# Reweaving the first mixer of a two-block fp32 network on one Trainium2 core

## The reference

```
mod = silu(c) @ w_ada + b_ada              # 6 vectors of 1024: shift1 scale1 gate1 shift2 scale2 gate2
h   = rms_norm(x, norm1_w) * (1 + scale1) + shift1
p   = h @ w_in
qkv = silu(causal_depthwise_conv(p[q, k, v columns], 4 taps))     # 4 heads of 128 each
g, beta = from two small groups of columns of p
o   = gated_delta_rule_chunked(l2_normalize(q), l2_normalize(k), v, g, beta)   # 8 chunks of 64 tokens
y_gdn = rms_norm(o, gdn_norm_w) * silu(z)                          # the output gate, 4 heads
y_sc  = sc_b * causal_depthwise_conv(sc_c * sc_h, 3 taps)          # short convolution half
x   = x + gate1 * (concatenate([y_gdn, y_sc]) @ w_out)
x   = x + gate2 * swiglu(rms_norm(x, norm2_w) * (1 + scale2) + shift2)
```

## Time and profile before

| | us |
|---|---|
| median of 3 runs | 2214.73 |
| the profiled execution, its own time | 2213.37 |
| its span, first to last instruction | 2212.1 |
| PE busy in the span | 2030.4 |
| DVE, ACT, POOL busy | 815.9, 694.8, 764.5 |
| mean granted clock of TensorE | 0.950 |

### The profile page before, as it was taken

How to read it: one execution, slowest core, us unless ns; L and a number is a source line. 1 busy time by engine, 2 the same in 40 slices (tenths; PEclk the granted TensorE clock), 3 DMA queues, 4 the chain that set the end, 5 groups by cost and what they waited for, 6 DMA issues and landing times. The chain is left out here.

```text
span 2212.1 us, 32165 instructions
## 1 busy us (share of the span) xinstructions
PE 2030.4 (92%) x13960; PEld 1697.1 (77%) x13960; DVE 815.9 (37%) x1075; ACT 694.8 (31%) x1048; POOL 764.5 (35%) x444
## 2 busy tenths in 40 slices
PE   3878999699999999999999888889999799999997
PEld 2656777578888889999999888776666577888885
DVE  5767362421111112443310266644444334444201
ACT  2342111343222233222222323344454324222222
POOL 2322120144444465344445432311111144444453
PEclk9988998799999999999999999889998999999999
DMA  7322221423333323323223422100000132333231
GB/s 266 133 96 77 77 77 39 135 76 103 92 93 92 97 86 96 96 89 93 84 90 93 130 67 72 39 6 2 1 2 2 64 118 86 96 95 95 88 95 64
DMA packets 55627, 182.76 MB, mean 83 GB/s; under 512 B 7456, under 2 KB 7712, under 8 KB 55360
## 3 DMA queue, kind: packets, MB, share of 16 engines
q1 hardware_dynamic: 55488, 180.72, 25.5%
HBM read 175.45 MB, written 5.24 MB: 82 GB/s over the span
## 5 line engine op out<-in xcount | busy, mean ns | idle before, releaser
L2076 POOL TENSOR_TENSOR WL<-RAWS,WH 128x1024 fp32r<-128x1024 f32 (+2 forms) x275 | 650.0, 2365 | 1032.2 <-ACT WH L1609 1032.2
L480 PE MATMUL PS<-HH,WH 128*128 128x264 f32 (+2 forms) x2184 | 681.8, 354 | 37.3 <-DVE HL L1028 7.5
L480 PE MATMUL PS<-HL,WH 128*128 128x264 f32 (+2 forms) x2184 | 661.4, 345 | 0.0
L480 PE MATMUL PS<-HH,WL 128*128 128x264 f32 (+2 forms) x2184 | 659.0, 344 | 0.0
L480 PEld LDWEIGHTS PS<-HH,WH 128*128 128x128 f32 (+1 forms) x2184 | 383.4, 193 | 106.6 <-issue 37.6
L1609 ACT ACTIVATE WH<-RAWS 128x1024 fp32r<-128x1024 f32 (+2 forms) x275 | 283.7, 1033 | 444.7 <-PE PS L480 429.4
L480 PEld LDWEIGHTS PS<-HH,WL 128*128 128x128 f32 (+1 forms) x2184 | 383.5, 193 | 49.2 <-issue 0.4
L480 PEld LDWEIGHTS PS<-HL,WH 128*128 128x128 f32 (+1 forms) x2184 | 383.8, 193 | 48.5 <-issue 3.4
L480 PE MATMUL PS<-IHf,WH 128*128 128x512 f32 (+1 forms) x704 | 209.4, 338 | 0.0
L480 PE MATMUL PS<-IHf,WL 128*128 128x512 f32 (+1 forms) x704 | 209.3, 338 | 0.0
L480 PE MATMUL PS<-ILf,WH 128*128 128x512 f32 (+1 forms) x704 | 209.2, 338 | 0.0
(11 more groups left out here) (499 smaller groups left out, 1981.1 us busy)
## 6 DMA issues: line engine op xcount, KB each, us to landing
RAWS<-w_w_in SPq DMA_DIRECT2D x52, 512.0 KB, 4.4
RAWS<-w_ada SPq DMA_DIRECT2D x32, 512.0 KB, 3.7
RAWS<-w_f0g SPq DMA_DIRECT2D x22, 512.0 KB, 3.6
RAWS<-w_f0u SPq DMA_DIRECT2D x22, 512.0 KB, 3.6
RAWS<-w_f1g SPq DMA_DIRECT2D x22, 512.0 KB, 3.6
RAWS<-w_f1u SPq DMA_DIRECT2D x22, 512.0 KB, 3.6
RAWS<-w_f2g SPq DMA_DIRECT2D x22, 512.0 KB, 3.6
RAWS<-w_f2u SPq DMA_DIRECT2D x22, 512.0 KB, 3.6
```

The costliest lines, as they stand in the source:

```text
L480: ins = te.matmul(ps[0:m, q, o:o + b - a] if len(halves) > 1 else ps[0:m, o:o + b - a], w[:, k * m:k * m + m], x[:, k0 + k, a:b], start=fi ...
L2076: ge.tensor_tensor(WL[s % NS][:, 0:n], RAW[i % NR][:, 0:n], WH[s % NS][:, 0:n].bitcast(f32), ALU.subtract).then_inc(*w_lo.up(s))
```

## The change

It touches the first mixer and the first feed-forward:

- The slabs of k and q come first (IN_ORDER: 4 to 7, then 0 to 3), then v. The Square of a head follows its Silu directly. The sums, roots and reciprocals of the l2 norm are made in two groups of four heads: the first after the convolution of the seventh slab, the second after that of the tenth.
- Slabs ten to 27 and the delta rule share the interleaved stretch. The delta rule's first tick comes after 30 empty ones. The ticks are dealt two pr, two dr, two pr, three dr. The interleaving therefore begins with two more slabs in it than before (18 instead of 16).
- Inside the delta rule three groups of matmuls are put in another order: the products of k and q alternate between the two halves of the output partitions, so do those of u, and the output of a chunk is made as four products of ST and then four of VN, not as four pairs.
- The output gate is made for each block of 128 tokens, in two ticks behind its `scan`. Its split into high and low part is made in two pieces at the end (PARTS).
- Half of the first two slabs of `w_out` (k-tiles 4 to 7, the short convolution) is done before the gated heads are there.
- The sixth vector of mod (8 `ada` slabs, gate2) moves into the first feed-forward, and the small work on the 16 meta tokens there moves ten steps later. Slabs of `ada` are loaded beside w_in in 24 places instead of 28.
- Half of the reload of X is issued earlier.

```diff
+DELTA_TICKS = 30
...
+IN_ORDER = [4, 5, 6, 7, 0, 1, 2, 3] + list(range(8, 28))
 ORDER = [("ab", 0, 512, True)]
-for _i in range(28):
-    ORDER += [("w_in", _i, SLAB, True), ("ada", 16 + _i, SLAB, False)]
-ORDER += [("ada", _i, SLAB, False) for _i in range(44, 48)]
+for _i, _j in enumerate(IN_ORDER):
+    ORDER += [("w_in", _j, SLAB, True)]
+    if _i < 24:
+        ORDER += [("ada", 16 + _i, SLAB, False)]
...
+        if _w == "f0" and 1 <= _j < 9:
+            ORDER += [("ada", 39 + _j, SLAB, False)]
...
-    SQB, SQT, L1R = (sbuf(x, [128, T2], st=mf) for x in ("SQB", "SQT", "L1R"))
+    SQB, SQL = sbuf("SQB", [128, T2], st=mf), sbuf("SQL", [128, 2 * T2], st=mf)
+    SQT, L1R = SQL[:, 0:T2], SQL[:, T2:2 * T2]
+    ACCS = [ACC[0], ACC[1], ACC[0], ACC[1], ACC[0], SQL[:, 0:SLAB]]
...
+    L2S = [XF[:, 512 * i:512 * i + 512] for i in range(8)]
+    PARTS = (slice(0, 384), slice(384, 512))
...
+        def l2_sums(i0):
+            for i in range(i0, i0 + 4):
+                if i in (4, 5):
+                    te.wait_ge(*l2_rt.at(i - 2))
+                te.wait_ge(*l2_sq.at(i))
+                te.matmul(bank(i if i0 else 2 + i), con("ones"), L2S[i], start=True, stop=True).then_inc(*l2_mm.up(i))
+
+        alternate(slab_gemm("ab", 0, main_bank("ab", 0), HH, HL, KT, H1, normed(0), m=64), project(IN_ORDER[0]))
+        for i in range(1, 10):
+            finish(project(IN_ORDER[i]))
+            if i == 2:
+                te.wait_ge(*row_d.at("rg"))
+                te.wait_ge(*row_a.at("beta"))
+                for n in range(4):
+                    ins = te.transpose(PS[:, 2, 64 * n:64 * n + 64], ROW[:, 128 * n:128 * n + 128],
+                                       con("ident")[0:64, 0:64])
+                ins.then_inc(*row_t.up(0))
+            elif i == 5:
+                te.wait_ge(*row_c.at("colt"))
+                l2_sums(0)
+        ada_column(2, main_bank("ada", 2))
+        l2_sums(4)
...
+            for i in range(10, 28):
+                yield from project(IN_ORDER[i])
+                if i in (17, 25):
+                    ada_column(3 + (i == 25), main_bank("ada", 3 + (i == 25)))
+                yield
+            for m in range(2):
+                out2.append(slab_gemm("w_out", m, main_bank("wo", m), HH, HL, KT, H1, joined1,
+                                      order=(4, 5, 6, 7, 0, 1, 2, 3)))
+            for _ in range(4):
+                for g in out2:
+                    next(g)
                 yield
...
             te.wait_ge(*d.at("kb", t))
-            for c, q in enumerate(HALF):
-                for h in range(4):
+            for h in range(4):
+                for c, q in enumerate(HALF):
                     t0 = 64 * (2 * b + c)
                     te.matmul(A[q, 64 * h:64 * h + 64], QKV[:, 4 + h, t0:t0 + 64], KB[e][:, h, 64 * c:64 * c + 64],
...
-            for q in HALF:
-                for h in range(4):
+            for h in range(4):
+                for q in HALF:
                     ins = te.matmul(A[q, 128 * h:128 * h + 128], XX[e][q, h, :], VBT[e][q, h, :], start=True, stop=True)
             ins.then_inc(*p.up("u", t))
...
                 for h in range(4):
-                    te.matmul(PS[:, 6, 64 * h:64 * h + 64], ST[:, h, :], QD[e][:, h, 64 * c:64 * c + 64], start=True,
-                              stop=False)
-                    ins = te.matmul(PS[:, 6, 64 * h:64 * h + 64], VN[q, h, :], AT[e][q, h, :], start=False, stop=True)
+                    te.matmul(PS[:, 6, 64 * h:64 * h + 64], ST[:, h, :], QD[e][:, h, 64 * c:64 * c + 64], start=h == 0,
+                              stop=False, skip_group_check=True)
+                for h in range(4):
+                    ins = te.matmul(PS[:, 6, 64 * h:64 * h + 64], VN[q, h, :], AT[e][q, h, :], start=False, stop=True,
+                                    skip_group_check=True)
                 ins.then_inc(*sp.up("o", n))
                 yield
...
+            te.wait_ge(*gt_sq.at(b))
+            te.matmul(bank(6), con("ones"), RSTD[:, 0:512], start=True, stop=True).then_inc(*gt_mm.up(b))
+            yield
+            yield
+
+        pr, dr = project_rest(), later_by(DELTA_TICKS, pipeline(4, prepare, scan))
+        alternate(pr, pr, dr, dr, pr, pr, dr, dr, dr)
+
+
+        alternate(*out2)
+        for m in range(2, 8):
+            if m >= 6:
+                te.wait_ge(*wo_x.at(m - 6))
+            finish(slab_gemm("w_out", m, wo_bank(m), HH, HL, KT, H1))
...
+                if f == 0 and job == 22:
+                    ada_column(5, bank(7))
...
+        def unit_heads(i0):
+            for i in range(i0, i0 + 4):
+                j = IN_ORDER[i]
+                ve.wait_ge(*l2_rt.at(i))
+                ve.reciprocal(L2S[i], L2S[i]).then_inc(*l2.up("rec", i))
+                ve.wait_ge(*l2.at("rec", i))
+                ve.scalar_tensor_tensor(QKV[:, j, :], QKV[:, j, :], 128.0 ** -0.5 if j < 4 else 1.0, L2S[i], ALU.mult,
+                                        ALU.mult).then_inc(*l2.up("mul", i))
...
+            convolve(i - 1)
+            if i == 3:
+                ve.wait_ge(*row_t.at(0))
+                ve.tensor_copy(COLT[:, :, :], h4(PS[:, 2, 0:256])).then_inc(*row_c.up("colt"))
+            elif i == 5:
+                ve.wait_ge(*row_e.at(0))
+                ve.tensor_tensor(BEG[:, :, :], EGC[:, :, :], COLT[:, :, 32:36], ALU.mult).then_inc(*row_c.up("beg"))
+            elif i == 7:
+                unit_heads(0)
+        ada(25)
+        convolve(9)
+        modulation(2, bank(MAIN_AT["ada", 2] % 2))
+        unit_heads(4)
...
+            o = OG[:, 0:4, 128 * b:128 * b + 128]
+            ve.wait_ge(*gt_r.at("exp", b))
+            ve.scalar_tensor_tensor(o, o, col("gdn"), h4(RSTD[:, 0:512]), ALU.mult, ALU.mult).then_inc(*gt_y.up("o", b))
+            ve.wait_ge(*gt_y.at("o", b))
+            ve.wait_ge(*zs.at(0))
+            ve.tensor_tensor(o, o, Z[:, :, 128 * b:128 * b + 128], ALU.mult).then_inc(*gt_y.up("z", b))
+            yield
+
+        def lower_gated(i):
+            ve.wait_ge(*gt_hi.at(i))
+            ve.tensor_tensor(HL[:, 0:4, NM:T2][:, :, PARTS[i]], OG[:, 0:4, PARTS[i]],
+                             HH[:, 0:4, NM:T2][:, :, PARTS[i]].bitcast(f32), ALU.subtract).then_inc(*gt_lo.up(i))
+
+        pr, dr = project_rest(), later_by(DELTA_TICKS, pipeline(4, prepare, scan))
+        alternate(pr, pr, dr, dr, pr, pr, dr, dr, dr)
+        for i in range(2):
+            lower_gated(i)
...
+                if f == 0 and 2 <= j < 10:
+                    ada(38 + j)
+                elif f == 0 and j == 11:
+                    modulation(5, bank(7))
+                if f == 0 and j == 12:
                     meta_tokens()
...
+            if i < 8:
+                ae.wait_ge(*cv_si.at(i))
+                ae.activation(L2S[i], QKV[:, j, :], ACT.Square).then_inc(*l2_sq.up(i))
+
+        def l2_roots(i0):
+            for i in range(i0, i0 + 4):
+                ae.wait_ge(*l2_mm.at(i))
+                ae.activation(L2S[i], bank(i if i0 else 2 + i), ACT.Sqrt, bias=EPSC[:, 0:1]).then_inc(*l2_rt.up(i))
...
+            elif i == 6:
+                l2_roots(0)
+        begin("w_in", IN_ORDER[10], 1)
+        convolve(9)
+        l2_roots(4)
...
+                    if u == 0:
+                        ae.wait_ge(*z_ev.at(3))
+                        ae.activation(Z[:, :, :], Z[:, :, :], ACT.Silu).then_inc(*zs.up(0))
+                        log_and_exp()
...
+            g = RSTD[:, 0:512]
+            ae.wait_ge(*so.at(2 * b + 1))
+            if b:
+                ae.wait_ge(*gt_y.at("o", b - 1))
+            ae.activation(h4(g), OG[:, 0:4, 128 * b:128 * b + 128], ACT.Square).then_inc(*gt_sq.up(b))
+            yield
+            ae.wait_ge(*gt_mm.at(b))
+            ae.activation(g, bank(6), ACT.Ln, bias=EPSC[:, 0:1], scale=1.0 / 128).then_inc(*gt_r.up("ln", b))
+            ae.wait_ge(*gt_r.at("ln", b))
+            ae.activation(g, g, ACT.Exp, scale=-0.5).then_inc(*gt_r.up("exp", b))
+            yield
+
+        def upper_gated(i):
+            ae.wait_ge(*gt_y.at("z", (2, 3)[i]))
+            ae.wait_ge(*gemm.at(CUT["w_in", 27]))
+            ae.activation(HH[:, 0:4, NM:T2][:, :, PARTS[i]], OG[:, 0:4, PARTS[i]], ACT.Copy).then_inc(*gt_hi.up(i))
...
+        se.wait_ge(*dp[1].at("qd", 1))
+        se.wait_ge(*pp[1].at("kq", 1))
+        se.dma_start(X[:, 4:8, NM:T2], xv[:, 4:8]).then_inc(s_x, 16)
+        se.dma_start(X[:, 4:8, 0:NM], mv[:, 4:8]).then_inc(s_x, 16)
         se.wait_ge(*sp.at("o", 7))
         se.wait_ge(*sd.at("st3", 7))
-        se.dma_start(X[:, :, NM:T2], xv).then_inc(s_x, 16)
-        se.dma_start(X[:, :, 0:NM], mv).then_inc(s_x, 16)
+        se.dma_start(X[:, 0:4, NM:T2], xv[:, 0:4]).then_inc(s_x, 16)
+        se.dma_start(X[:, 0:4, 0:NM], mv[:, 0:4]).then_inc(s_x, 16)
```

(55 more changed lines are left out.)

326 lines of the change are left out of this document (101 added, 225 removed).

## The result

The changed kernel takes 2197.43 us (median of 4 runs, 2196.09 to 2201.10), the kernel before on the same chip 2214.98 (4 runs): ratio 0.992, 95% interval 0.990 to 0.994. The gain is 17.5 us where 37 were forecast: the time lies in the range, but the gain is less than half of what was forecast.

The account below looks back on a forecast made before the run. TensorE (PE), busy 2030 of 2212 us, was taken as the bound. Late start +7.3, stretch -22.3, slabs +4.9, tail -29.2 made -39.3; feed-forward +2.3 gave -37.0: 2178 us, range 2162 to 2204.

Parts of the forecast that it names:

- part 1: Convolutions and heads' norm, before the first k and q products: 7.3 us late and half a slab behind, +10.0.
- the halves of k, q and u: Interleaved stretch: alternating array halves saves 1.9 us on the k and q products and 2.0 on u.
- The output, the first step that failed: Interleaved stretch: grouping each chunk's eight output products takes them from 2.9 to 1.1 us, gain 14.4 over 8 chunks.
- The clock: Interleaved stretch: of 14.1 us lost to low PE clock, 5 stay as the slow output products shrink, -9.1.
- Rival A: Shape change is not what costs: output products keep 0.36 each, pairs give nothing, low clock stays; 2206, chance 0.12.
- B: PE is kept full: no clock lost, idle as before, the norm at a third of its bound; 2164, chance 0.15.
- The reweaving in the stretch: Interleaved stretch: more slabs +4.9, three gate sums +3.1, fewer shape changes -4.4, more PE idle time +6.4.
- gate sums: Interleaved stretch: three of the four output gate sums move in, 1.02 us each, +3.1.
- pairs: Interleaved stretch: dealing slab ticks in twos saves 22 pairs of changes between slab and small matmuls, 0.2 each, -4.4.
- Parts 3 and 4: Mixer's tail after the last chunk's output: 52.2 us instead of 81.4; first feed-forward with the sixth mod vector: +2.3.
- Rival C: Back-to-back delta rule ticks expose the hand-over, 1.3 us for each of 48 groups; 2234, chance 0.05.
- rival D: Sparse last chunks and two holes before the stretch at half clock, PE idle 25 us in it; 2196, chance 0.13.

Follow-up runs that it names:

- e5_pe_order: Kernel before with only three TensorE loops reordered: output products grouped, halves of k, q and u in turn, nothing rewoven; 2194.87 us.
- e10_grouped: Kernel before with only the chunk's output products grouped, nothing rewoven; 2201.19 us.
- e6_log_norm: Changed kernel with the heads' norm by ACT's Ln and Exp in place of ACT's Sqrt and DVE's reciprocal; 2179.19 us.
- e4_split_output: Changed kernel with each output product cut into two of 64 weight columns, alternating between the array's column halves; 2187.89 us.
- e2_old_halves: Changed kernel with the products of k and q and of u again one half of the array after the other; 2205.01 us.
- e3_single_ticks: Changed kernel with the old deal of ticks, one slab tick and one delta rule tick in turn; 2203.32 us.
- e11_spread: Changed kernel with Ln and Exp norm, output products cut in two, and the short convolution's taps one to a tick on DVE; 2163.68 us.
- e1_old_output: Changed kernel with the chunk's output in the old order, per head the ST product, then the VN one; 2213.48 us.

## Why the prediction was half right

Direction and range held, and of part 1 the marks; the size of the gain did not. At the mixer's end I had -39.3: -27.4 for the three loops of PE with the clock they give back, -11.9 for the reweaving. Measured with e5_pe_order between the two kernels: -18.4 and -0.9. With e10_grouped as well it splits further: the output with its clock -12.1 where I had -23.5, the halves of k, q and u -6.3 where I had -3.9, the reweaving -0.9 where I had -11.9. So two steps failed, by 11.4 and 11.0: the price of the output's products, and what the reweaving costs in the stretch and ahead of it.

- **Part 1.** Silus at 110.0, 121.0, 142.3, 150.7 and 157.3 (forecast 110.0, 121.1, 141, 149.5, 156), slab 12 at 184.1 (182.7), k and q at 203.0 (200.0). The sum is 3.0 short. The holes of PE were shared out wrongly: 14.1 and 17.6 where I had some 7 and 24. That it is the reciprocals, behind which ACT and PE stand, e6_log_norm shows.
- **The output, the first step that failed.** "So most of 0.36 is the change between 128x128 and 64x128 ... I count 8 x 0.12 and one change of 0.2: 1.1." Measured 2.07: I had 0.97 too little in each chunk, 7.8 in all. Of the 0.36 the change of shape is 0.14, not most of it, and the product 0.22, not 0.12. I took 0.12 from the products of k and q as the price of 64 moving columns. Those have 64 weight columns; the output's have 128, and e4_split_output shows that it was the weight columns: cut to 64 the price falls with them. The term was 6.6 at full clock (2.9 less 2.07, by 8), not 14.4. The state's update just ahead of it had the price: 1.08 for four products of 128 weight columns, one change of shape among them. Nor were seven changes replaced by one: eight were replaced by two.
- The Trainium skill, TensorE: Matmul & The Clock Gate, "LDWEIGHTS (loading the stationary operand)", says that a weight load goes by its columns, whatever the rows. The traces agree: of the output's loads those with 128 columns take 192 ns in the median with 128 rows and 188 with 64, those with 64 columns in e4_split_output 138. The load records are longer than that section's P / 1.2, an estimate of 107 ns for 128 columns, but the records inside a run follow each other every 0.11 us (0.67 for six). The rule spoke against my 0.12, and I did not weigh it.
- **The clock.** Counted as a term of its own (-9.1), with the loops' terms beside it. It is not one, since the clock goes with each loop: with the old output the new weave loses 24.2, grouped 8.3, split 3.5; with the old halves 15.5. How much clock a loop gives back depends on the rest. Put into the old weave, the output gave 12.1 and the halves on top of it 6.3; taken back in the new weave, the output cost 17.6 and the halves 11.1, together more than the whole change gained. The parts don't add up, and the total of the loops in the old weave, 18.4, is what can be compared with my 27.4.
- **Rivals A and B.** Rival A (the shape change is not what costs) is wrong: a change costs 0.14, and the first product behind the state's update pays it without a shared sum. B (PE kept full) is out by the 17.4 idle and 8.3 slow clock in the stretch.
- **k, q and u.** 1.9 + 2.0 forecast; by the rows of e2_old_halves against the changed kernel 2.7 + 2.0, and clock besides. The trace bears out the Trainium skill's rule, TensorEngine Tiling (Array Packing), "Key Properties", of two 128x64 tiles at once: 0.06 instead of 0.12.
- **The reweaving in the stretch, the second step that failed.** Forecast +10.0 (4.9 of slabs, 3.1 of gate sums, -4.4 of pairs, +6.4 idle). Measured against e5_pe_order +14.4: work +2.0 (5.1 of slabs and 3.1 of sums less 6.2, about what e3_single_ticks gives the pairs), idle +9.2, slow clock +3.2. The idle time was named but sized at two thirds, and the clock that sparse work costs was left out. PE's largest waits there are for DVE: one of 4.1 behind the taps (shown above), 3.4 for VN, most of it in the sparse end, and 2.0 in another inverse; for each of these e5_pe_order waits 0.9 at most. Why DVE is late there is not settled beyond the taps: the pairs of ticks make 3.4 of it, and e11_spread took back less than 2. Ahead of the stretch the reweaving lost 11.0 against e5_pe_order where I had 7.3, and in the tail it won 26.3 where I had 29.2.
- **Parts 3 and 4.** The tail is 54.4 against 52.2 forecast; the wait for the short convolution and its split is 1.6 of it (forecast 2.5). Part 4 cost 2.0 against 2.3.

The miss of 20.0 at the mixer's end is thus 3.0 of a late start, 14.8 of the stretch (184.7 forecast, 199.5 measured) and 2.2 of the tail. In the stretch the terms that were mis-sized are the output's products (6.6 for 14.4), PE's idle time (17.4 for 12) and the slow clock (8.3 for the 5.0 that the forecast left): 16.5 together, less 1.7 in small terms the other way. Rival C did not happen. The time came out at rival D's (2196), and in part for its reason, since the sparse end has clock 0.62. But idle time was 17.4 where D has 25, and D holds nothing of the 7.8 that the output lacks: that its time is met is luck.

## What to carry to other kernels

Take a product's price from a row with as many weight columns, not only as many moving ones, and take the price of a change of shape apart from it: here 128 weight columns cost 0.22 us and 64 cost 0.12 with the same 64 moving columns, and a change 0.14. Before a schedule is rewoven, put the loops of the bounding engine in a better order by themselves and time that: here three loops gave all that the whole change gave. Look for the slowest block that a weave queues in one piece: with four reciprocals in a row this one gained nothing, with Ln and Exp in their place 16 us.

## What the runs showed of the chip

- Small f32 products at full clock, for one product inside a run of its shape: 64 weight and 64 moving columns 0.12 us, 0.06 with the other column half in turn; 128 and 64 0.22. Each change between products with all rows and with half the rows adds 0.14, so that the two in turn start 0.36 apart, with as many weight columns.
- TensorE's granted clock falls inside a run of such alternating products while PE shows no idle time (368.7 in e1_old_output); in the changed kernel, with the same products grouped, the clock stays at its upper level from 203 to 330. Grouping alone is no warrant of it: e10_grouped still loses 10.3 us in the stretch. Which property of the products decides, no run here tells apart.
- The norm of 128x512 values: DVE's reciprocal 3.35 us. Replacing eight of them by ACT's Ln and Exp moved the start of the delta rule by 21.5 us.
